# Down weights of the feed-forward stages issued by ScalarE, one transfer a row

## What is computed

```
def swiglu(n, w_gate, w_up, w_down):          # n: 256 x 1024
    return (silu(n @ w_gate) * (n @ w_up)) @ w_down
# w_gate, w_up: 1024 x 2816;  w_down: 2816 x 1024
```

## Time and profile before

| | us |
|---|---|
| median of three runs (1515.71 to 1520.01) | 1518.47 |
| span of the profiled execution, first to last instruction | 1516.6 |
| TensorE busy with matmuls | 1435.0 (95%) |
| VectorE busy | 861.4 (57%) |
| ScalarE busy | 756.3 (50%) |

### The profile page before, as it was taken

How to read it: one execution, slowest core, us unless ns; L and a number is a source line. 1 busy time by engine, 2 the same in 40 slices (tenths; PEclk the granted TensorE clock), 3 DMA queues, 4 the chain that set the end, 5 groups by cost and what they waited for, 6 DMA issues and landing times.

```text
span 1516.6 us, 19819 instructions
## 1 busy us (share of the span) xinstructions
PE 1435.0 (95%) x6476; PEld 1168.8 (77%) x6476; DVE 861.4 (57%) x1328; ACT 756.3 (50%) x1233; POOL 61.7 (4%) x92
## 2 busy tenths in 40 slices
PE   7999999989999998999999989999999989999998
PEld 5877778777878787787777778878787767888887
DVE  6455556866545556555464665555653754565554
ACT  6444456534544546554454564455554633455543
POOL 0000010400000001000000000000100100000000
PEclk9999999999999999999998999999998967999999
DMA  8555546545555564555553155545474620455553
GB/s 267 181 180 180 180 153 210 171 153 166 167 194 192 168 199 133 175 166 188 188 199 105 56 184 165 191 167 166 155 207 139 211 84 28 139 180 181 166 183 122
DMA packets 199327, 251.65 MB, mean 166 GB/s; under 512 B 19718, under 2 KB 138084, under 8 KB 199276
## 3 DMA queue, kind: packets, MB, share of 16 engines
q1 hardware_dynamic: 199152, 250.97, 51.0%
q10 hardware_dynamic: 124, 0.03, 0.0%
HBM read 249.89 MB, written 1.05 MB: 165 GB/s over the span
## 4 chain that ended last, share of the span: by engine, by line
PE 54%; DVE 13%; DMA 13%; SPq 7%; issue 7%; ACT 5%; POOL 0%; DVEq 0%; ACTq 0%
PE ps L1635 16%; PE ps L1637 15%; PE ps L1636 15%; DMA raw<-in_ffn_w_up 10%; DVE wlo L1007 7%; SPq L309 6%; DVE wlo L1015 4%; ACT whi L546 3%; PE ps L1661 2%; DMA raw<-in_w_up 2%; DVE hid L1032 1%; DMA raw<-in_w_in 1%; PE ps L1747 1%; ACT whi L550 1%; PE ps L2144 1%
## 5 line engine op out<-in xcount | busy, mean ns | idle before, releaser
L1007 DVE SCALAR_TENSOR_TENSOR wlo<-raw,gcol,whi 128x512 fp32r<-128x512 f32 (+1 forms) x600 | 434.7, 772 | 427.2 <-ACT whi L546 422.0
L546 ACT ACTIVATE whi<-raw,gcol 128x512 fp32r<-128x512 f32 (+1 forms) x600 | 397.0, 714 | 427.0 <-DMA raw<-in_ffn_w_up 288.2
L1635 PE MATMUL ps<-whi,kthi 128*128 128x512 f32 (+2 forms) x1400 | 561.0, 401 | 23.9 <-DVE wlo L1007 12.4
L1636 PE MATMUL ps<-wlo,kthi 128*128 128x512 f32 (+2 forms) x1400 | 549.8, 393 | 0.0
L1637 PE MATMUL ps<-whi,ktlo 128*128 128x512 f32 (+2 forms) x1400 | 549.7, 393 | 0.0
L1635 PEld LDWEIGHTS ps<-whi,kthi 128*128 128x128 f32 x1400 | 270.4, 193 | 82.7 <-issue 14.7
L1637 PEld LDWEIGHTS ps<-whi,ktlo 128*128 128x128 f32 x1400 | 270.1, 193 | 55.7
L1636 PEld LDWEIGHTS ps<-wlo,kthi 128*128 128x128 f32 x1400 | 270.6, 193 | 51.4
L1015 DVE TENSOR_TENSOR wlo<-raw,whi 128x1024 fp32r<-128x1024 f32 x151 | 179.3, 1214 | 56.9 <-ACT whi L550 55.9
L550 ACT CAST whi<-raw 128x1024 fp32r<-128x1024 f32 x151 | 152.9, 1043 | 69.9 <-PE ps L1637 58.7
L1635 PE MATMUL ps<-whi,hthi 128*128 128x512 f32 x440 | 172.0, 391 | 0.0
(11 more groups left out here) (192 smaller groups left out, 730.8 us busy)
## 6 DMA issues: line engine op xcount, KB each, us to landing
raw<-in_ffn_w_gate SPq DMA_DIRECT2D x176, 256.0 KB, 4.8
raw<-in_ffn_w_up SPq DMA_DIRECT2D x176, 256.0 KB, 5.5
raw<-in_ffn_w_down SPq DMA_DIRECT2D x176, 256.0 KB, 3.3
raw<-in_w_in SPq DMA_DIRECT2D x80, 256.0 KB, 3.7
raw<-in_gmlp_w_in SPq DMA_DIRECT2D x64, 256.0 KB, 3.2
raw<-in_w_gate SPq DMA_DIRECT2D x44, 256.0 KB, 4.5
raw<-in_w_up SPq DMA_DIRECT2D x44, 256.0 KB, 5.3
raw<-in_w_down SPq DMA_DIRECT2D x44, 256.0 KB, 3.3
```

The costliest lines, as they stand in the source:

```text
L546: ins = nc.scalar.activation(whi[:, s, cut], raw[:, s, cut], ACT.Copy, scale=gcol[:, k:k + 1])
L1007: ins = nc.vector.scalar_tensor_tensor(out=wlo[:, s, cut], in0=raw[:, s, cut], scalar=gcol[:, k:k + 1], in1=f32(whi[:, s, cut]), op0=ALU.m ...
L1635: nc.tensor.matmul(dst, lhs[0], rhs[0], start=first, stop=False)
L1636: nc.tensor.matmul(dst, lhs[0], rhs[1], start=False, stop=False)
```

## The change

SyncE's loop no longer has the down rows of tiles 1 to 10; it keeps those of tile 0, which it issues ahead of the loop. ScalarE has a new function `down_rows(j)`: for slot 4 and then slot 5 it waits until `lo_done` says that the slot's tile before has been split, and issues the slot's 128 x 1024 numbers as one 512 KB transfer that adds 32 to `raw_in`. Before, they were two of 256 KB that added 16 each. ScalarE calls it first thing in each pass of its loop (tiles 1 to 9) and once after the loop (tile 10). SyncE's transfers of `between` stay where they were.

```
-                base = [n - 1 for n in use]
+                base = [n - 1 for n in use[:4]]
                 parts = len(between) + 1
                 for part in range(parts):
                     with sp.Fori(1 + part * (NF - 1) // parts, 1 + (part + 1) * (NF - 1) // parts) as j:
                         for s in range(4):
                             gate_up(s, j + base[s], gate, up, j * FT)
-                        for f in range(2):
-                            rows(4 + f, j + base[4 + f], down, j * 2 + f)
...
-            def ffn_rest(name, pre, then=None):
+            def ffn_rest(name, pre, w_down, then=None):
                 base, b = [n - 1 for n in use], seen.get("hid_full", 0)
+                down = w_down.rearrange("(c p) n -> p c n", p=P)
+
+                def down_rows(j):
+                    for f in range(2):
+                        s = 4 + f
+                        act.wait_ge(lo_done[s], j + base[s])
+                        act.dma_start(raw[:, s, :], down[:, bass.ds(j * 2 + f, 1), :].rearrange("p c n -> p (c n)")
+                                      ).then_inc(raw_in[s], 32)
...
                 turned_hidden(0)
                 with act.Fori(1, NF - 1) as j:
+                    down_rows(j)
                     for s in range(3):
                         high(s, j + base[s], name)
...
                     turned_hidden(j)
+                down_rows(NF - 1)
                 for s in range(SLOTS):
                     use[s] += NF - 2
```

More of the change, by code:

```diff
@@ L761, in _ @@
             act.wait_ge(sem("gcol_ready"), 2)
-            ffn_rest("ffn00", "pre_ffn00", following("mix0"))
+            ffn_rest("ffn00", "pre_ffn00", a["ffn_w_down"][0, 0], following("mix0"))
             after_ffn("post_ffn00", "pre_mix0", latest(5))
@@ L784, in _ @@
             ffn_first("ffn01", "pre_ffn01")
-            ffn_rest("ffn01", "pre_ffn01", following("kv", R_KV + ROPE))
+            ffn_rest("ffn01", "pre_ffn01", a["ffn_w_down"][0, 1], following("kv", R_KV + ROPE))
             after_ffn("post_ffn01", "pre_kv", latest(5))
@@ L828, in _ @@
             more(3)
-            ffn_rest("ffn10", "pre_kv", following("mix1"))
+            ffn_rest("ffn10", "pre_kv", a["ffn_w_down"][1, 0], following("mix1"))
             after_ffn("post_ffn10", "pre_mix1", latest(5))
@@ L919, in _ @@
             ffn_first("ffn11", "pre_ffn11")
-            ffn_rest("ffn11", "pre_ffn11", following("mix2"))
+            ffn_rest("ffn11", "pre_ffn11", a["ffn_w_down"][1, 1], following("mix2"))
             after_ffn("post_ffn11", "pre_mix2", latest(5))
@@ L974, in _ @@
             ffn_first("ffn2", "pre_ffn2")
-            ffn_rest("ffn2", "pre_ffn2")
+            ffn_rest("ffn2", "pre_ffn2", a["w_down_2"][0])
         @block.vector
```

## The result

The changed kernel takes 1491.12 us (median of 4 runs, 1488.67 to 1495.15) against 1517.19 us beside it: a ratio of 0.9837, 95% interval 0.9803 to 0.9871. 1492 had been forecast.

The account below looks back on a forecast made before the run. TensorE, busy 95% of the span, was taken as the bound, gains coming only from its stalls. The 1516.6 us span less 26.7 gives 1489.9; runs' median lies 1.9 above: 1491.8, given as 1492, range 1486 to 1506.

Parts of the forecast that it names:

- Where the 26.7 us were: Five seven-tile feed-forward stretches exceed their 117.6 us floor by 26.7 us in all; all of it goes.
- rival B: Tiles with a transfer of `between` stay late: 21.3 us of stall stay, only 5.4 go; 1513 us, chance 0.09.
- Why gate and up were late: In SyncE's queue they stood behind the down rows' wait; slot 0's gate left 8.9 us after it could have.
- Rival C: ScalarE's wait takes the place of SyncE's, so highs start as late as before; no change, 1518 us, chance 0.05.
- ScalarE's two issues: Ahead of ScalarE's highs each tile: 0.5 us each with its wait, first high 3.8 us after the transposes, no cost.
- Rival D: ScalarE is held in its two issues, costing once one takes over 3.7 us; 1542 us at 4.3 us, chance 0.05.
- The slack: In a loop tile, ScalarE's first high may come up to 10.2 us after the transposes before TensorE stalls.
- One transfer for two: One 512 KB row transfer for two of 256 KB lands within 6.7 us; effect nothing, bounds -0.3 to +0.3 us.
- Rival A: Only issue time is saved on SyncE: gate and up leave 1.98 us earlier; gain 24 us, 1494.5 us, chance 0.09.
- The other 25 tiles ... all given back: With only issue time saved, 25 tiles holding 5.4 us in stalls under 2 us each lose all those stalls.
- Clock: Half-speed matmuls after stalls, about 3 us within the 26.7, go; pieces between stages may shift time 3 us either way.
- The Trainium skill's rule: Issuing from several engines saves only the sequencer's time to start transfers, usually small; here put at 1.98 us a tile.

Follow-up runs that it names:

- order-only version: Kernel before with only SyncE's order changed: down rows of a tile stand behind gate and up of the next, SyncE keeping all transfers; 1484.38 us, ratio 0.9791.
- one-transfer version: Kernel before with SyncE issuing each slot's down rows, in the old place, as one 512 KB transfer instead of two of 256 KB; 1503.94 us, ratio 0.9926.
- With the wait kept: Changed kernel, but from tile 3 SyncE holds slot 0's gate and up until VectorE finished the second row slot of the tile before last; 1501.39 us, ratio 0.9901.
- mended stage end: Changed kernel with stage end reordered: next stage's slots 0 and 1, last SiLU half and product, slot 2, last turned half, slot 3; 1493.07 us, ratio 0.9850.
- three versions with another stage end: Last SiLU half and product before next stage's slot 2, on the changed kernel 1494.23 us, with rows reordered on SyncE 1495.67; slot 3 also moved last, 1493.07.
- third series: Changed kernel unaltered, run again beside a version with another stage end on the same chip; 1484.45 us, ratio 0.9802 to the kernel before.
- first stage-end version: Changed kernel with the last SiLU half and its product moved before slot 2 of the next stage on ScalarE and VectorE; 1494.23 us, ratio 0.9851.

## Why the prediction was right

The mechanism was right in kind and in size, and the experiments bear it out. That the first series came within 0.9 us of the forecast is in part luck: the parts between the stages move the same kernel by 6 to 7 us. The steps, in its order:

- **Where the 26.7 us were.** Right: 614.74 to 588.13 us in the five stretches, 26.6. The floor of 16.80 us a tile holds for all of the loops' tiles, also next to the transfers of `between`, so rival B (1513) did not come.
- **Why gate and up were late.** Right, and shown rather than argued by the order-only version: the wait in front of them in an in-order queue was the cause. Rival C fell with it; ScalarE waited 0.9 us for the second row slot (930.99 to 931.94), where 1.0 had been counted.
- **ScalarE's two issues.** Taken at 0.5 us each, measured at 0.36 (all 100 of them between 0.358 and 0.391). The first is issued while ScalarE's arithmetic still runs, at 930.28, ahead of the cast at 930.41 that precedes it in the program. The first high stands at 3.5 us instead of 3.8, but for another reason than the count gave: it waits for TensorE's slot, and it stands at 3.5 us too in the order-only version, where ScalarE waits for no rows and issues none. Rival D's issue of over 3.7 us never occurred; its decision point was tested by holding ScalarE longer and came out at 1.0 us a tile where 1.1 was counted.
- **The slack.** 10.2 us after the transposes as the edge: no loss with the high at 7.3, 0.7 us with it at 10.98, 1.0 with it at 11.5. What was missed is the first pass of each stage, where the room is smaller: holding ScalarE 4.3 us costs 1.0 us there, 7.5 us over 4. In the changed kernel that pass is on time.
- **One transfer for two.** Nothing on ScalarE, as taken. On SyncE in its old place it is worth a third (medians) to a half (profile) of the gain, but through the shorter queue. The 6.7 us that the prediction takes as the latest landing is the median of four transfers of norm gains and no bound; no run needed it.
- **Rival A rests on a step that does not hold everywhere.** It gave back 24 of 26.7 us for gate leaving 2 us earlier, and treated the time of issue as all that the rows take from gate and up. No run has its exact condition. The one-transfer version agrees with its rule: 0.4 to 1.1 us a stalled tile, and 13.8 of 26.6 us back. With the wait kept, SyncE issues no rows and gate leaves only 0.6 us earlier, counted from the transposes; 12.3 us of stalls stood there. "The other 25 tiles ... all given back" fails in that run: stage 5, all small stalls, went from 1.2 to 4.9 us over its floor, as the transfers took longer once issued.
- **Clock.** The two half-clock pieces inside the loops are gone, as said. That pieces between the stages may come or go was right in kind, but 3 us either way was too small: the changed kernel's own profiles lie 6.9 us apart. The sum counts 26.7 us of gain, and the five stretches hold 26.6; side by side with the kernel before, the three series of the changed kernel gained 26.1, 34.6 and 31.6 us. The 5 to 8 us beyond the stretches were not foreseen.

The Trainium skill's rule, page "DMA: Bandwidth & Descriptors", section "Issuing engines are not separate DMA queues", is borne out by these runs as far as it goes: the order-only version on one engine equals the change on two, so the second issuer gave nothing that the order did not. What it says of the time saved, only the start of a transfer, is not all that went here: in the tiles of the earlier trace rows and of the changed kernel's tile shown above, gate's lateness behind its own low went from 8.9 to 0.2 us, most of it a wait.

## What to carry to other kernels

A queue that starts transfers in program order should have them in the order in which their buffers come free. Here the wait for the last slot of one tile delayed the four slots of the next, the first of them by 8.9 us, and putting the rows one tile later in the same queue is worth as much as giving them to another engine. Before a new instruction is put on an engine, count how late its next result may be; in this kernel the record of a tile without a stall gave that edge within 0.3 us. Look at the first pass of a loop by itself, where the cover can be thinner.

## What the runs showed of the hardware

The time outside the stretches depends on half-clock pieces that the same kernel gets in one run and not in another. The part from the last transposes of stage 3 to the first of stage 4, in the kernel before, in the changed kernel's first profile, in its third, and with the mended stage end (length, busy times, granted clock third from the end):

```profile
787.03:908.46 121.43, 109.77 (x549) 87.67 (x549) 75.83 (x159) 64.05 (x129) 8.81 (x24) 0.94 0.35 113
```

```profile
762.54:884.24 121.70, 110.05 (x548) 87.95 (x549) 75.84 (x159) 64.04 (x129) 8.77 (x24) 0.94 0.32 104
```

```profile
763.62:879.20 115.58, 103.95 (x548) 82.97 (x549) 75.79 (x159) 64.00 (x129) 8.76 (x24) 1.00 0.35 110
```

```profile
765.06:887.62 122.56, 109.32 (x550) 87.94 (x550) 77.16 (x161) 65.62 (x132) 8.77 (x24) 0.94 0.33 105
```

The same 548 matmuls take 6.1 us more where the clock is 0.94 of full (part of the time at its 1.2 GHz level); TensorE's idle time is the same, 11.6 us in both. This one part holds 6.1 of the 6.9 us between the changed kernel's profiles of 1488.0 and 1481.1 us, and 7.0 of the 10.2 us by which the mended stage end is behind.

Over 16 runs the changed kernel falls in two groups: eight of 1483 to 1485 us with a mean clock of 0.975 or 0.976, and eight of 1487 to 1495 with 0.967 to 0.972. Which group a run falls in is not chance alone. Of the kernel before, 2 of 46 runs had a mean clock of 0.973 or more, and its profile has the longer form of the part above; of the three versions with another stage end, none of 17 runs had more than 0.971. So a change in one place can shift the clock in another. Between the profiles of the kernel before and of the changed kernel's third series lie 35.5 us, 8.9 more than in the stretches, and 5.9 of these 8.9 stand in this one part.

TensorE had been waiting before such pieces wherever I looked: 2.88 us before 170.50 in the kernel before, 1.93 us before 199.04 in the first stage-end version. But a wait is not always followed by one (2.48 us of idle before 496.83 in the kernel before, with full clock after). What tips it was not found. A change worth under 0.5% in this kernel can be hidden or faked by it, and only the busy stretches tell.
